# A two-network transformer kernel: where the activation tiles lie against the weight tiles, modulo 256 bytes

## Chip, cores and metric

The kernel runs on one core of one Trainium2 chip, in one launch. The metric is the device time of that launch in microseconds; the figure compared is the median of several runs.

## What is computed

Two networks run one after the other on 256 tokens of width 1024, all in float32, two layers each. Cut to what matters here:

```python
# first network, per layer (256 latent tokens; in layer 0 also 256 context tokens)
h = modulate(rmsnorm(x, norm1_g), sh1, sc1)
p = h @ w_in                                  # conv input, q, k, v, gates
y_conv = conv_branch(p[..., :GLU_END])        # depthwise conv, layernorm, silu, @ w_conv_out
y_attn = neighbourhood_attention(q, k, v) @ w_na_out
x = x + g1 * ((g_conv * y_conv + g_attn * y_attn) @ w_out)
h2 = modulate(rmsnorm(x, norm2_g), sh2, sc2)
x = x + g2 * ((silu(g) * a) @ w_down)         # a, g from dwconv(h2 @ w_up)
# second network, per layer (16 meta tokens + the 256 tokens)
u = rmsnorm_2(h) ; proj = u @ w_in
h = h + concat(indexer_attention, diff_attention, retention) @ w_out
u = rmsnorm_2(h) ; h = h + square(relu(u @ w_ff1)) @ w_ff2
```

## The kernel before

Every linear layer is done in split precision. Each float32 operand is cut into a rounded part (`_hi`) and the rest (`_lo`), and a product is three TensorE matmuls: high weights by high activations (L1369), high weights by low activations (L1370), low weights by high activations (L1374). Each of the three loads its own 128x128 weight tile and then streams 256, 272 or 512 activation columns past it. While one matmul streams, TensorE loads the weight tile of the next.

The weights come as a stream of 442 slabs of 128x1024 numbers (512 KB). A slab passes four engines, in a ring of four slots: SyncE starts its DMA into `raw`; ScalarE rounds it into `w_hi` (L846); GpSimd subtracts to get `w_lo`, in two halves (L803); TensorE uses both. TensorE's release of a slab (`slab_used`) lets ScalarE overwrite the slot of `w_hi` four slabs on, GpSimd's release (`w_lo_ready`) lets the next DMA into `raw` start. Most slabs of the first network are used by `chunk` (L1380) or `up` (L1748): for eight pieces k of the width first the L1369/L1370 pair, and when `w_lo` of the slab is there eight times L1374, so 24 matmuls a slab.

Stages of the first network, in order of time: input projection, `qk` and values of layer 0 (h, 512 columns, up to 171 us), attention of layer 0 with the gate chunks put between its steps by a table (171 to 312), the two branches (`at`, `cv`), the output mix (`y`), the up projection (`h`), the down projection (`dn`, to 766 us); then the same for layer 1 with 256 columns, apart from its key and value chunks that still have 512. In layer 1 the down projection reads `fa`. The second network starts at about 1208 us and uses `u`, `o`, `v`, `f`.

The tiles of SBUF are placed by hand: `sb` takes the next free address of a partition, rounded up to 32 bytes, `at` puts a name on any address. What counts for this change is an address modulo 256. The weight tiles of the first network (`w_hi0`, `w_lo0`) start at 128 modulo 256, and so does every 128x128 piece of them, since pieces are 512 bytes apart. In the second network the weight area has 64 bytes more in each row of pieces (`TURN`), so that successive k start 64 bytes further, as its activations of 272 columns (1088 bytes) do. Before the change a few tiles were already placed by hand 64 bytes short of the weight tiles modulo 256: `fa_hi`, `fa_lo`, and in layer 1 the copies `as_*`, `cs_*` of `at_*`, `cv_*`:

```python
fa_hi = at("fa_hi", [FF_C, SEQ], F32R, g_at + 192)
attns = [(at_hi, at_lo), (shifted("as_hi", QC, q_at, 192), shifted("as_lo", QC, q_at + QC * T_BOTH * 4, 192))]
```

Of the kernel before, what the change touches and what calls it, by code (L numbers as in the profile page):

```python
# [18 lines left out]
F32 = mybir.dt.float32  # L19
# [93 lines left out]
_n = 0  # L113
for _name, _w in (("ident", P), ("ones_d", P), ("ones_c", P), ("ones_h", P), ("perm1", P), ("perm2", P),
                  ("sel", 8), ("hsel", 16), ("sums", 2), ("cos1", SEQ), ("sin1", SEQ), ("win", GRID_W),
                  ("cos2", T2), ("sin2", T2), ("causal", N1 + N2), ("decay", 4 * 512),
                  ("onehot", VLEN), ("vmask", VLEN)):
    TAB[_name] = (_n, _n + _w)
    _n += _w
# [7 lines left out]
def build(nc, A, out, marks):  # L127
# [44 lines left out]
    with ctx:  # L172
# [28 lines left out]
        w_lo = [weight_area(f"w_lo{n}", w_at + w_size, turn) for n, turn in enumerate((0, TURN))]  # L201
        cst = sb("cst", [6 * P + 26])
        prm = sb("prm", [DEPTH, PRM1_N])
# [37 lines left out]
        x_at = top[0]  # L241
        X = sb("X", [DC, T_BOTH])
        h_at = top[0]
        h_hi = sb("h_hi", [DC, T_BOTH], F32R)
# [7 lines left out]
        ffa = at("ffa", [FF_C, T_BOTH], F32, g_at)  # L252
        fa_hi = at("fa_hi", [FF_C, SEQ], F32R, g_at + 192)
        fa_lo = at("fa_lo", [FF_C, SEQ], F32R, g_at + 192 + FF_C * SEQ * 4)
        q_at = top[0]
# [8 lines left out]
        upad = sb("upad", [CONV_C, 2, SEQ + 2 * HALO])  # L264
        top[0] += (128 - top[0]) % 256
        cv_at = top[0]
# [4 lines left out]

        def shifted(name, rows, o, by):
            return at(name, [rows, T_BOTH], F32R, o + by)[:, :, 0:SEQ]

        attns = [(at_hi, at_lo), (shifted("as_hi", QC, q_at, 192), shifted("as_lo", QC, q_at + QC * T_BOTH * 4, 192))]
        convs = [(cv_hi, cv_lo), (shifted("cs_hi", CONV_C, up_at, 192), shifted("cs_lo", CONV_C, cv_at, 192))]
        bias_at = top[0]
# [16 lines left out]
        assert 192 + 3 * DC * T2 * 4 + 4096 <= 2 * DC * T_BOTH * 4  # L294
        tab2 = at("tab2", [2 * T2 + N1 + N2 + 4 * 512], F32, x_at)
# [26 lines left out]
        assert o + 1536 + 3 * T2 * 4 <= end1, (o, end1)  # L322
        assert g_at + 192 + 2 * FF2_C * T2 * 4 <= o

# [17 lines left out]
        ident = cst[:, 0:P]  # L342
        ones_d, ones_c, ones_h = (cst[:, i * P:(i + 1) * P] for i in (1, 2, 3))
        perm1, perm2, sel = cst[:, 4 * P:5 * P], cst[:, 5 * P:6 * P], cst[:, 6 * P:6 * P + 8]
        hsel = cst[:, 6 * P + 8:6 * P + 24]
        sums = cst[:, 6 * P + 24:6 * P + 26]

# [486 lines left out]
        def _(act):  # L834
# [90 lines left out]
            def network1(layer):  # L925
# [27 lines left out]
                def attend(kind, n, *others):  # L953
# [20 lines left out]
                    elif kind == "Tx":  # L974
                        if n >= 2:
                            act.wait_ge(*after("attn_pv", (layer, n // 2 - 1)))
                        for t in range(2):
                            act.wait_ge(*after("attn_turned", (layer, n, t)))
                            copy(pt_x[n % 2][:, :, t * P:(t + 1) * P], bank[sx_bank(n, t)][:, :].rearrange("p (k q) -> p k q", k=4))\
                                .then_inc(*done("attn_pt", (layer, n, t)))  # L980
                    elif kind == "Tc" and layer == 0:
                        act.wait_ge(*after("attn_turned", (layer, n, 2)))
                        copy(pt_c[n % 2][:, :, :].rearrange("p k (t q) -> p t k q", t=2),
                             aux[2][:, :].rearrange("p (t k q) -> p t k q", t=2, k=2))\
                            .then_inc(*done("attn_pt", (layer, n, 2)))
                    elif kind == "mean":
                        for c in range(CONV_C):
                            act.wait_ge(*after("conv_centred", (layer, c)))
                            act.activation(conv_sq(c)[:, 0:T], cv[:, c, 0:T], ACT.Square).then_inc(*done("ln_sq", (layer, c)))
                    elif kind == "V":  # L990
                        act.wait_ge(*after("attn_pv", (layer, n)))
                        copy(attns[layer][0][:, n, 0:T], aux[3][:, 0:T]).then_inc(*done("attn_hi", (layer, n)))
                    elif kind == "var":

                        ahead(s + 2 * DC)
# [48 lines left out]
                for c in range(CONV_C + 1):  # L1044
# [3 lines left out]
                    if c:  # L1048
                        act.wait_ge(*after("conv_silu", (layer, c - 1)))
                        copy(convs[layer][0][:, c - 1, 0:T], nb[:, c - 1, 0:T]).then_inc(*done("conv_hi", (layer, c - 1)))  # L1050

# [294 lines left out]
        def _(pe):  # L1346
# [247 lines left out]
            def network1(layer):  # L1594
# [108 lines left out]
                def attention_branch(m):  # L1703
# [4 lines left out]
                    for k in range(4):  # L1708
                        three(bank[m % 4][:, 0:T], s + m, 4 + k, attns[layer][0][:, k, 0:T], attns[layer][1][:, k, 0:T], k == 0, k == 3)

                def conv_branch(m):
                    b = 4 + m % 4
                    claim(b)
                    for k in range(4):
                        if m == 0:
                            pe.wait_ge(*after("conv_lo", (layer, k)))
                        mm = three(bank[b][:, 0:T], s + m, k, convs[layer][0][:, k, 0:T], convs[layer][1][:, k, 0:T], k == 0, k == 3)
                    mm.then_inc(*done("slab_used", s + m))
# [529 lines left out]
        def _(dve):  # L2248
# [137 lines left out]
            def network1(layer):  # L2386
# [106 lines left out]
                def rest(p):  # L2493

                    dve.wait_ge(*after("attn_hi", (layer, p)))
                    tt(attns[layer][1][:, p, 0:T], aux[3][:, 0:T], attns[layer][0][:, p, 0:T].bitcast(F32), ALU.subtract)\
                        .then_inc(*done("attn_lo", (layer, p)))
# [51 lines left out]
                for c in range(CONV_C + 2):  # L2549
# [10 lines left out]
                    if c >= 2:  # L2560
                        dve.wait_ge(*after("conv_hi", (layer, c - 2)))
                        tt(convs[layer][1][:, c - 2, 0:T], nb[:, c - 2, 0:T], convs[layer][0][:, c - 2, 0:T].bitcast(F32), ALU.subtract)\
                            .then_inc(*done("conv_lo", (layer, c - 2)))
# [446 lines left out]
def shape_tables():  # L3010
# [9 lines left out]
    put("ones_c", np.full((P, P), 1 / (CONV_C * P)))  # L3020
    put("ones_h", (i[:, None] // HD == i[None, :] // HD) / HD)
    for name, half in (("perm1", 16), ("perm2", 32)):
# [190 lines left out]
```

## Time and profile before

| what | value |
|---|---|
| runs of the kernel before | 1958.83, 1959.35, 1960.12 us; median 1959.35 |
| profiled execution, first to last instruction | 1959.9 us (the page gives this span, and no other time of that execution; it lies 0.5 above the median, inside the three runs) |
| TensorE busy | 1904.2 us, 12126 matmuls |
| GpSimd busy | 1187.7 us |
| VectorE busy | 1065.5 us |
| ScalarE busy | 891.8 us |
| mean granted TensorE clock | 0.994 |

Matmuls overlap in the profile: the next one starts long before the modelled end of the one ahead. So the duration of a matmul isn't its price; the price is the distance from start to start, called pitch below. Engines that wait show idle time in front of an instruction and the name of what ended it; a short stall of TensorE inside a stream of matmuls shows only as a longer pitch.

### The profile page before, as it was taken

How to read it: one execution, taken by the hardware profiler on the slowest of the kernel's cores; microseconds unless marked ns; L12 is line 12 of the kernel's file. 1: busy time of each engine (PE TensorE's matmuls, PEld its weight loads, DVE VectorE, ACT ScalarE, POOL GpSimd, SP SyncE). 2: the span in 40 equal slices, each digit the busy share in tenths (PEclk: the TensorE clock that was granted, in tenths of full speed). 3: DMA queues.
4: the chain of work that ended last, by engine and by line, in shares of the span. 5: the costliest groups of instructions: out<-in, count | busy, mean ns of one | idle time of the engine just before them, and what ended most of it. 6: DMA issues, size and time to landing. Idle time of an engine off the chain costs nothing.

```text
span 1959.9 us, 33261 instructions
## 1 busy us (share of the span) xinstructions
PE 1904.2 (97%) x12126; PEld 1624.1 (83%) x12126; DVE 1065.5 (54%) x1972; ACT 891.8 (46%) x1520; POOL 1187.7 (61%) x904
## 2 busy tenths in 40 slices
PE   7999999999999999999899999999999999999998
PEld 4677777888888887877889999787999998769987
DVE  4899865354443324887657744876542048555400
ACT  4223444243443323525546645556554355555533
POOL 2444233424654554635469987674788876649986
PEclk9999999999999999999999999999999999999999
DMA  9942233628433343436465575432455564326554
GB/s 387 362 127 76 56 96 117 228 78 172 147 107 107 120 149 121 150 91 211 139 204 172 182 230 182 164 108 89 130 183 182 173 206 139 109 75 205 185 179 130
DMA packets 121541, 307.04 MB, mean 157 GB/s; under 512 B 29640, under 2 KB 51528, under 8 KB 121044
## 3 DMA queue, kind: packets, MB, share of 16 engines
q1 hardware_dynamic: 118808, 300.98, 46.8%
q10 hardware_dynamic: 2620, 4.51, 1.5%
q8 instruction: 77, 1.26, 0.3%
q14 instruction: 36, 0.29, 0.0%
HBM read 300.72 MB, written 8.06 MB: 158 GB/s over the span
## 4 chain that ended last, share of the span: by engine, by line
issue 36%; POOL 31%; PE 28%; DVE 4%; ACT 1%; POOLq 0%; ACTq 0%; DVEq 0%
POOL w_lo L803 30%; PE bank L1369 7%; PE bank L1374 6%; PE bank L1370 6%; PE bank L2081 2%; PE bank L2082 2%; PE bank L2083 2%; DVE nb L2258 1%; PE bank L1966 1%; PE bank L1968 1%; PE bank L1967 1%; ACT w_hi L846 0%; DVE v_lo L2258 0%; PE bank L2185 0%; DVE v_lo L2250 0%
## 5 line engine op out<-in xcount | busy, mean ns | idle before, releaser
L803 POOL TENSOR_TENSOR w_lo<-raw,w_hi 128x512 fp32r<-128x512 f32 x884 | 1169.7, 1353 | 759.4 <-ACT w_hi L846 757.2
L846 ACT ACTIVATE w_hi<-raw 128x1024 fp32r<-128x1024 f32 x442 | 466.1, 1056 | 285.2 <-PE bank L1374 146.8
L1369 PE MATMUL bank<-h_hi,w_hi 128*128 128x256 f32 (+1 forms) x1248 | 407.4, 342 | 1.8 <-DVE h_lo L2258 1.1
L1370 PE MATMUL bank<-h_lo,w_hi 128*128 128x256 f32 (+1 forms) x1248 | 399.4, 336 | 0.0
L1369 PEld LDWEIGHTS bank<-h_hi,w_hi 128*128 128x128 f32 x1248 | 237.2, 190 | 43.0 <-issue 13.2
L1374 PE MATMUL bank<-h_hi,w_lo 128*128 128x256 f32 (+1 forms) x1248 | 262.8, 335 | 0.0
L1370 PEld LDWEIGHTS bank<-h_lo,w_hi 128*128 128x128 f32 x1248 | 237.3, 190 | 23.6 <-issue 0.2
L1374 PEld LDWEIGHTS bank<-h_hi,w_lo 128*128 128x128 f32 x1248 | 204.7, 190 | 23.9
L1369 PE MATMUL bank<-u_hi,w_hi 128*128 128x272 f32 (+1 forms) x736 | 212.0, 288 | 1.1 <-DVE u_lo L2258 1.1
L1374 PE MATMUL bank<-u_hi,w_lo 128*128 128x272 f32 (+1 forms) x736 | 209.1, 284 | 0.0
L1370 PE MATMUL bank<-u_lo,w_hi 128*128 128x272 f32 (+1 forms) x736 | 208.3, 283 | 0.0
L1369 PEld LDWEIGHTS bank<-u_hi,w_hi 128*128 128x128 f32 x736 | 138.7, 188 | 5.5 <-issue 3.6
L1370 PEld LDWEIGHTS bank<-u_lo,w_hi 128*128 128x128 f32 x736 | 138.9, 189 | 0.1
L1374 PEld LDWEIGHTS bank<-u_hi,w_lo 128*128 128x128 f32 x736 | 138.9, 189 | 0.0
L2258 DVE SCALAR_TENSOR_TENSOR cv<-upad,prm,cv 128x512 f32<-128x512 f32 x120 | 129.0, 1075 | 3.6
L2258 DVE SCALAR_TENSOR_TENSOR up_g<-bank,prm,up_g 128x510 f32<-128x510 f32 (+1 forms) x88 | 54.2, 616 | 82.4 <-ACT up_g L1088 76.3
L2258 DVE SCALAR_TENSOR_TENSOR up_a<-bank,prm,up_a 128x510 f32<-128x510 f32 (+1 forms) x88 | 54.1, 614 | 56.4 <-ACT up_a L1088 50.4
L2250 DVE TENSOR_TENSOR bank<-bank,sq 128x272 f32<-128x272 f32 (+1 forms) x76 | 33.4, 440 | 93.3 <-ACT up_t L1296 93.2
L1369 PE MATMUL bank<-f_hi,w_hi 128*128 128x272 f32 x256 | 73.8, 288 | 0.0
L1374 PE MATMUL bank<-f_hi,w_lo 128*128 128x272 f32 x256 | 73.8, 288 | 0.0
L2258 DVE SCALAR_TENSOR_TENSOR X<-bank,gh,X 128x256 f32<-128x256 f32 x48 | 21.6, 479 | 95.3 <-PE bank L1374 95.3
L1370 PE MATMUL bank<-f_lo,w_hi 128*128 128x272 f32 x256 | 72.9, 285 | 0.0
(394 smaller groups left out, 3720.8 us busy)
## 6 DMA issues: line engine op xcount, KB each, us to landing
raw<-in_wstream SPq DMA_DIRECT2D x442, 512.0 KB, 3.5
ada_raw<-in_wada SPq DMA_DIRECT2D x48, 512.0 KB, 13.1
late_a<-in_wada SPq DMA_DIRECT2D x16, 512.0 KB, 5.1
late_b<-in_wada SPq DMA_DIRECT2D x16, 512.0 KB, 4.5
biash<-rpb_by_offset SPq DMA_DIRECT2D x64, 64.0 KB, 2.5
gates<-in_wada SPq DMA_DIRECT2D x8, 512.0 KB, 5.0
rpb_by_offset<-in_rpb SPq DMA_DIRECT2D x16, 224.0 KB
bias_by_distance<-vec ACTq DMA_DIRECT2D x1, 3264.0 KB
```

Source lines behind the costliest of these rows:

```text
L803: i = pool.tensor_tensor(lo[:, part, s, :], whole[:, part, :], hi[:, part, s, :].bitcast(F32), ALU.subtract)
L846: act.activation(w_hi[q >= first["l2", 0]][:, :, s, :], raw[:, s, :].rearrange("p (g c) -> p g c", c=PAIR), ACT.Copy)\
L1369: pe.matmul(o, tile(w_hi, i, k), a_hi, start=start, stop=False)
L1370: pe.matmul(o, tile(w_hi, i, k), a_lo, start=False, stop=False)
L1374: return pe.matmul(o, tile(w_lo, i, k), a_hi, start=False, stop=stop)
L1966: pe.matmul(lin[b][:, :], a, wh, start=kk == 0, stop=False)
L1967: pe.matmul(lin[b][:, :], al, wh, start=False, stop=False)
L2081: pe.matmul(o[:, :], hi, wh, start=j == 0, stop=False)
L2082: pe.matmul(o[:, :], lo, wh, start=False, stop=False)
L2083: return pe.matmul(o[:, :], hi, wl, start=False, stop=j == FF2_C - 1)
L2250: return dve.tensor_tensor(o, a, b, op)
L2258: return dve.scalar_tensor_tensor(out=o, in0=a, scalar=s, in1=b, op0=op0, op1=op1)
```

## The change

The constant table `ones_h` is no longer loaded (nothing read it), so `cst` is 512 bytes shorter in each partition and everything behind it starts 512 bytes lower, which changes nothing modulo 256. Then three places round the next free address up to 64 bytes short of the weight tiles modulo 256, and what was shifted by hand before is shifted no more. No instruction is added, removed or moved on any engine: the program differs in the addresses and in the width of one DMA (`cst`, 794 numbers a partition before, 666 now).

```diff
-for _name, _w in (("ident", P), ("ones_d", P), ("ones_c", P), ("ones_h", P), ("perm1", P), ("perm2", P),
+for _name, _w in (("ident", P), ("ones_d", P), ("ones_c", P), ("perm1", P), ("perm2", P),
...
-        cst = sb("cst", [6 * P + 26])
+        cst = sb("cst", [5 * P + 26])
...
         X = sb("X", [DC, T_BOTH])
+        top[0] += (w_at - 64 - top[0]) % 256
         h_at = top[0]
...
-        fa_hi = at("fa_hi", [FF_C, SEQ], F32R, g_at + 192)
-        fa_lo = at("fa_lo", [FF_C, SEQ], F32R, g_at + 192 + FF_C * SEQ * 4)
+        fa_hi = at("fa_hi", [FF_C, SEQ], F32R, g_at)
+        fa_lo = at("fa_lo", [FF_C, SEQ], F32R, g_at + FF_C * SEQ * 4)
...
-        top[0] += (128 - top[0]) % 256
+        top[0] += (w_at - 64 - top[0]) % 256
         cv_at = top[0]
...
-        attns = [(at_hi, at_lo), (shifted("as_hi", QC, q_at, 192), shifted("as_lo", QC, q_at + QC * T_BOTH * 4, 192))]
-        convs = [(cv_hi, cv_lo), (shifted("cs_hi", CONV_C, up_at, 192), shifted("cs_lo", CONV_C, cv_at, 192))]
...
         o = h_at
-        o += 192
         ffn_in = [tuple(at(f"u_{part}{l}", [DC, T2], F32R, o + by + n * DC * T2 * 4) for n, part in enumerate(("hi", "lo")))
-                  for l, by in enumerate((0, -192))]
+                  for l, by in enumerate((0, 64))]
+        o += 64
...
-                   for l, (n_mid, by) in enumerate(((T2, 192), (SEQ, 0)))]
+                   for l, (n_mid, by) in enumerate(((T2, 0), (SEQ, 64)))]
         o += (L2_FRONT * T2 + 3 * 1024) * 4
+        o += (w_at - 64 - o) % 256
```

`attns[layer][0]`, `convs[layer][0]` and their like become `at_hi`, `cv_hi` where they are used. What the code gives for the start addresses modulo 256 (the first network's weight tiles are at 128 in both; "moving" is the operand that streams):

| tile | used as | before | now |
|---|---|---|---|
| `h`, `y`; `at`, `cv` in layer 0 | moving, 256 or 512 columns | 128 | 64 |
| `h` in the value projection (L1657 to L1659) | stationary, weights move | 128 | 64 |
| `at`, `cv` in layer 1 (`as`, `cs` before) | moving, 256 columns | 64 | 64 |
| `fa` | moving, 256 columns | 64 | 64 |
| `dn` | moving, 512 columns | 128 | 128 |
| second network: `u` of its two layers | moving, 272 or 256 columns | 64, 128 | 64, 128 |
| second network: `f`; `o`, `v` of layer 0; `o` of layer 1 | | 64, 128; 64; 0 | the same |
| `qT`, `kT`, `V`, `cv`, `gates`, `pj`, the `late` loads, `ada_raw` | float32 matmuls, vector work, DMA | 128 | 64 |
| second network: `V2` | float32 matmuls | 64 | 0 |

## Rows read from the trace of the kernel before

**Rows 1.** The page, part 1: span, TensorE's busy time.

```profile
span 1959.9 us, 33261 instructions
...
PE 1904.2 (97%) x12126; PEld 1624.1 (83%) x12126; DVE 1065.5 (54%) x1972; ACT 891.8 (46%) x1520; POOL 1187.7 (61%) x904
```

**Rows 2.** Windows by stage: PE, PEld, DVE, ACT, POOL busy (instructions), PEclk, DMA, GB/s.

```profile
0.00:55.00 55.00, 40.84 (x216) 26.23 (x216) 27.49 (x56) 22.04 (x37) 10.89 (x12) 0.97 0.99 389
55.00:171.00 116.00, 116.00 (x568) 85.28 (x560) 106.00 (x132) 28.48 (x36) 59.01 (x38) 1.00 0.57 195
171.00:312.00 141.00, 135.43 (x648) 99.84 (x647) 99.00 (x176) 65.01 (x133) 46.01 (x33) 0.99 0.27 78
438.00:656.00 218.00, 218.00 (x965) 180.57 (x966) 95.32 (x129) 85.01 (x106) 114.00 (x84) 1.00 0.47 130
874.00:955.00 81.00, 75.27 (x551) 63.60 (x551) 58.72 (x128) 45.60 (x91) 41.87 (x32) 0.98 0.59 196
1031.00:1147.00 116.00, 116.00 (x969) 116.00 (x969) 86.54 (x145) 72.76 (x122) 105.70 (x81) 1.00 0.57 181
1147.00:1208.00 61.00, 60.24 (x528) 59.85 (x527) 15.82 (x19) 24.41 (x27) 55.00 (x44) 1.00 0.75 236
...
1777.00:1861.00 84.00, 84.00 (x719) 83.92 (x719) 38.71 (x94) 48.33 (x90) 76.90 (x62) 1.00 0.61 197
```

**Rows 3.** Timeline of TensorE: start, us, instruction; matmuls of one low-weight run merged.

```profile
599.91 1.98 PE L1374 MATMUL bank<-h_hi,w_lo 128*128 128x512 f32 x8
...
605.35 0.84 PE L1374 MATMUL bank<-h_hi,w_lo 128*128 128x512 f32 x3
...
1099.99 1.12 PE L1374 MATMUL bank<-h_hi,w_lo 128*128 128x256 f32 x8
...
1102.87 0.40 PE L1374 MATMUL bank<-h_hi,w_lo 128*128 128x256 f32 x2
...
1182.86 1.07 PE L1374 MATMUL bank<-fa_hi,w_lo 128*128 128x256 f32 x8
...
1185.58 0.62 PE L1374 MATMUL bank<-fa_hi,w_lo 128*128 128x256 f32 x4
```

**Rows 4.** Groups by line and form: count, busy us, mean ns of one, idle before.

```profile
L1374 PE MATMUL bank<-h_hi,w_lo 128*128 128x512 f32 x608 | 154.8, 389 | 0.0
...
L1374 PE MATMUL bank<-u_hi,w_lo 128*128 128x272 f32 x416 | 119.9, 288 | 0.0
...
L1374 PE MATMUL bank<-h_hi,w_lo 128*128 128x256 f32 x640 | 108.0, 283 | 0.0
...
L2081 PE MATMUL bank<-w_hi,f_hi 128*128 128x512 f32 x128 | 50.6, 396 | 0.0
...
L1370 PE MATMUL bank<-fa_lo,w_hi 128*128 128x256 f32 x176 | 41.0, 276 | 0.0
...
L1966 PE MATMUL bank<-w_hi,u_hi 128*128 128x512 f32 x96 | 39.4, 411 | 0.1
...
L1657 PE MATMUL bank<-w_hi,h_hi 128*128 128x512 f32 x64 | 26.0, 406 | 0.0
...
L1370 PE MATMUL bank<-as_lo,w_hi 128*128 128x256 f32 x32 | 8.8, 276 | 0.0
```

**Rows 5.** The page, part 5: the weight loads of the low-weight matmuls on h.

```profile
L1374 PEld LDWEIGHTS bank<-h_hi,w_lo 128*128 128x128 f32 x1248 | 204.7, 190 | 23.9
```

**Rows 6.** What TensorE waited for in each attention: us in total, times, longest.

```profile
PE bank L1891 <- DVE p_x L2254: 2.2, 1, 2.2
...
PE bank L1891 <- DVE sq L2254: 4.5, 6, 1.0
```

**Rows 7.** Issues of the constant table: KB, us to landing.

```profile
cst<-in_tables ACTq DMA_DIRECT2D x1, 397.0 KB, 6.5
```

**Rows 8.** GpSimd's group in the up projection of layer 1, 1031 to 1147 us.

```profile
L803 POOL TENSOR_TENSOR w_lo<-raw,w_hi 128x512 fp32r<-128x512 f32 x81 | 106.4, 1348 | 10.3 <-ACT w_hi L846 10.3
```

**Rows 9.** A window of the first attention: columns as in Rows 2.

```profile
186.00:190.00 4.00, 3.04 (x15) 2.42 (x16) 3.82 (x10) 1.82 (x4) 0.37 (x1) 0.73 0.90 344
```

More of the change, by code:

```diff
@@ L270, in build @@
         cv_lo = at("cv_lo", [CONV_C, T_BOTH], F32R, cv_at)
-        def shifted(name, rows, o, by):
-            return at(name, [rows, T_BOTH], F32R, o + by)[:, :, 0:SEQ]
-        attns = [(at_hi, at_lo), (shifted("as_hi", QC, q_at, 192), shifted("as_lo", QC, q_at + QC * T_BOTH * 4, 192))]
-        convs = [(cv_hi, cv_lo), (shifted("cs_hi", CONV_C, up_at, 192), shifted("cs_lo", CONV_C, cv_at, 192))]
         bias_at = top[0]
@@ L288, in build @@
         o = h_at
-        o += 192
         ffn_in = [tuple(at(f"u_{part}{l}", [DC, T2], F32R, o + by + n * DC * T2 * 4) for n, part in enumerate(("hi", "lo")))
-                  for l, by in enumerate((0, -192))]
+                  for l, by in enumerate((0, 64))]
+        o += 64
         H = at("H", [DC, T2], F32, o + 2 * DC * T2 * 4)
         pt_odd = at("pt_odd", [2, 512], F32, o + 3 * DC * T2 * 4)
-        assert 192 + 3 * DC * T2 * 4 + 4096 <= 2 * DC * T_BOTH * 4
+        assert 64 + 3 * DC * T2 * 4 + 4096 <= 2 * DC * T_BOTH * 4
         tab2 = at("tab2", [2 * T2 + N1 + N2 + 4 * 512], F32, x_at)
@@ L322, in build @@
         assert o + 1536 + 3 * T2 * 4 <= end1, (o, end1)
-        assert g_at + 192 + 2 * FF2_C * T2 * 4 <= o
+        assert g_at + 64 + 2 * FF2_C * T2 * 4 <= o
         KI, QI, QCR, KCR, QB, KB, QA, KA, GC = 0, 1, 5, 7, 9, 11, 13, 17, 21
@@ L342, in build @@
         ident = cst[:, 0:P]
[L343 to L346, printed above, removed]
+        ones_d, ones_c = (cst[:, i * P:(i + 1) * P] for i in (1, 2))
+        perm1, perm2, sel = cst[:, 3 * P:4 * P], cst[:, 4 * P:5 * P], cst[:, 5 * P:5 * P + 8]
+        hsel = cst[:, 5 * P + 8:5 * P + 24]
+        sums = cst[:, 5 * P + 24:5 * P + 26]
         by_distance = nc.dram_tensor("bias_by_distance", (A_HEADS + B_HEADS, P, VLEN), F32).ap()
@@ L991, in attend @@
                         act.wait_ge(*after("attn_pv", (layer, n)))
-                        copy(attns[layer][0][:, n, 0:T], aux[3][:, 0:T]).then_inc(*done("attn_hi", (layer, n)))
+                        copy(at_hi[:, n, 0:T], aux[3][:, 0:T]).then_inc(*done("attn_hi", (layer, n)))
                     elif kind == "var":
@@ L1049, in network1 @@
                         act.wait_ge(*after("conv_silu", (layer, c - 1)))
-                        copy(convs[layer][0][:, c - 1, 0:T], nb[:, c - 1, 0:T]).then_inc(*done("conv_hi", (layer, c - 1)))
+                        copy(cv_hi[:, c - 1, 0:T], nb[:, c - 1, 0:T]).then_inc(*done("conv_hi", (layer, c - 1)))
                 for m in range(DC):
@@ L1708, in attention_branch @@
                     for k in range(4):
-                        three(bank[m % 4][:, 0:T], s + m, 4 + k, attns[layer][0][:, k, 0:T], attns[layer][1][:, k, 0:T], k == 0, k == 3)
+                        three(bank[m % 4][:, 0:T], s + m, 4 + k, at_hi[:, k, 0:T], at_lo[:, k, 0:T], k == 0, k == 3)
                 def conv_branch(m):
@@ L1716, in conv_branch @@
                             pe.wait_ge(*after("conv_lo", (layer, k)))
-                        mm = three(bank[b][:, 0:T], s + m, k, convs[layer][0][:, k, 0:T], convs[layer][1][:, k, 0:T], k == 0, k == 3)
+                        mm = three(bank[b][:, 0:T], s + m, k, cv_hi[:, k, 0:T], cv_lo[:, k, 0:T], k == 0, k == 3)
                     mm.then_inc(*done("slab_used", s + m))
@@ L2495, in rest @@
                     dve.wait_ge(*after("attn_hi", (layer, p)))
-                    tt(attns[layer][1][:, p, 0:T], aux[3][:, 0:T], attns[layer][0][:, p, 0:T].bitcast(F32), ALU.subtract)\
+                    tt(at_lo[:, p, 0:T], aux[3][:, 0:T], at_hi[:, p, 0:T].bitcast(F32), ALU.subtract)\
                         .then_inc(*done("attn_lo", (layer, p)))
@@ L2561, in network1 @@
                         dve.wait_ge(*after("conv_hi", (layer, c - 2)))
-                        tt(convs[layer][1][:, c - 2, 0:T], nb[:, c - 2, 0:T], convs[layer][0][:, c - 2, 0:T].bitcast(F32), ALU.subtract)\
+                        tt(cv_lo[:, c - 2, 0:T], nb[:, c - 2, 0:T], cv_hi[:, c - 2, 0:T].bitcast(F32), ALU.subtract)\
                             .then_inc(*done("conv_lo", (layer, c - 2)))
@@ L3020, in shape_tables @@
     put("ones_c", np.full((P, P), 1 / (CONV_C * P)))
-    put("ones_h", (i[:, None] // HD == i[None, :] // HD) / HD)
     for name, half in (("perm1", 16), ("perm2", 32)):
```

## The prediction

> **What bounds the kernel now.** I read the busy times first: TensorE is busy 1904.2 of 1959.9 us [rows 1], far ahead of GpSimd, so time comes only from TensorE's stream or from its few waits. Next the windows by stage [rows 2]: in the long stages of the first network (438 to 656, 1031 to 1147 us) TensorE is busy for the whole window at a granted clock of 1.00, that is 2.4 GHz, and waits for nothing. There the only question is how far apart matmuls start.
>
> The timeline answers that [rows 3]. From one run of L1374 to the next are 24 matmuls, one slab. On h with 512 columns that takes 605.35 - 599.91 = 5.44 us, a pitch of 226.7 ns; on h with 256 columns 2.88 us, 120.0 ns; on fa with 256 columns 2.72 us, 113.3 ns. At 2.4 GHz the columns alone take 213.3 and 106.7 ns, so h pays 13.3 ns over them at both widths, and fa 6.7. The h and fa matmuls of 256 columns have the same shape, type, line and order of passes. What differs is the place: h starts at the weight tiles' own address modulo 256, fa 64 bytes before it. The durations say the same [rows 4]: 283 ns for h, 276 for fa, and also 276 for as, which a different line of code placed at the same 64 bytes. So it is the place, not the tile.
>
> While a matmul streams, the weights of the next are loaded: one load lasts 190 ns in the mean [rows 5], longer than a pitch of 113 to 120 ns, so loading and streaming read memory side by side all the time. My reading is that two streams that start at the same address modulo 256 get in each other's way once per matmul, for 6.7 ns (16 columns at 2.4 GHz, which are 64 bytes), and that 64 bytes less avoids it.
>
> The Trainium skill ("SBUF — State Buffer", section "Who interferes with whom") says against this that TensorE has two independent read ports, one for moving data and one for weight loads, and waits for no one. By that rule addresses cost nothing and the change is worth nothing; the trace disagrees at 256 columns, 120.0 against 113.3 ns, and is silent at 512.
>
> **The change part by part.** The moved tiles are h, y, and at and cv of layer 0. Per slab 24 matmuls change place. Counting with the code: at 256 columns h has 3 x 640 and y 3 x 64 = 2112 together; at 512 columns h has 3 x 608, y 3 x 64, at and cv 3 x 32 each, 2208 together (640 and 608 are in [rows 4]).
>
> *256 columns.* Price measured, 6.7 ns. Of the 2112, 1728 lie in the up projection of layer 1 (1056), the first slabs of layer 0's up projection (192), layer 1's projections (288) and its mix (192), where TensorE hardly waits: 1728 x 6.7 ns = 11.6 us. The other 384 are the gate chunks in the attention of layer 1, where TensorE is busy 75.27 of 81 us [rows 2]. They fill time between steps that end with VectorE, six of the waits for it being the 4.5 us of [rows 6]: a chunk that is done sooner then only makes the next wait longer. Of 2.6 us I take half, 1.3, with 0 and 2.6 as ends.
>
> *512 columns.* No 512-column group of the first network lies anywhere but at distance zero, so this price isn't in the trace. Its bounds: 6.7 ns if the overhead falls to that of fa; a loss if it becomes like the 512-column rows of the second network, 396 ns (L2081) and 411 ns (L1966) against 389 for h [rows 4]. I take 6.7, because the overhead over the columns is the same 13.3 ns at both widths, and because the weight load is as long as before while the streaming is longer, so that the first half of a 512-column matmul meets what a 256-column one meets. Of the 2208, 1440 lie in stages where TensorE is the bound (960 up projection of layer 0, 192 mix, 192 branches, 96 keys of layer 1): 9.6 us. 384 are the first projections of layer 0: a quarter of them runs before 55 us, where TensorE is busy only 40.84 of 55 us and the DMA engines 0.99 [rows 2], and is worth nothing; the others lie where TensorE is busy 116 of 116 us: 288 x 6.7 ns = 1.9 us. 384 are gate chunks of the first attention, busy 135.43 of 141 us, with a single wait of 2.2 us as the largest [rows 6]: of 2.6 us I take 1.5.
>
> *The value projection* (L1657 to L1659, 3 x 64 matmuls) has h as the weights, so it goes to 64 bytes on the other side. The nearest row is the up stage of the second network's layer 1, whose first two passes stream 64 bytes past their weights: 719 matmuls in 84.00 us [rows 2], 116.8 ns, 10.2 over the columns, 3 better than now. 192 x 3 ns = 0.6 us gained; ends 1.3 gained (6.7 each) and 1.3 lost (7 each, as L2081 against h).
>
> *Nothing or nearly:* fa, at and cv of layer 1, dn, u, f, o and v keep their address modulo 256. qT and kT move together. Vector, ScalarE and GpSimd operations and DMAs keep their multiples of 64 bytes; I take 0 for them. The constant load is 397 KB [rows 7] and loses 64; at the 389 GB/s of the first window [rows 2] that is 0.17 us in a DMA-bound start, of which 0.1 counted.
>
> *What is late next.* TensorE's slab in the up projection of layer 1 comes down to 24 x 113.3 ns = 2.72 us. GpSimd needs, for its two halves, 106.4 us / 40.5 slabs = 2.63 us [rows 8], 3% less, and now has 10.3 us of waits in that window to give. So it still covers, just; the fa stage shows that it can: 60.24 of 61 us busy at 113.3 ns [rows 2], though there with little VectorE work beside it. I take 1.0 us lost, between 0 and the 1056 x 6.7 ns = 7.1 us of the stage if GpSimd were the bound. The granted clock is 0.73 in a window of the first attention that follows a wait [rows 9]; about a quarter of 4 us, 1 us, is what such a drop costs. One more or one less: 0, ends -1 and +1.
>
> Sum: 11.6 + 1.3 + 9.6 + 1.9 + 1.5 + 0.6 + 0.1 - 1.0 = 25.6 us. The profiled execution's span of 1959.9 us goes to 1934.3; it lies 0.55 above the median of 1959.35, so the median goes to 1933.8. With every term at its best end (11.6 + 2.6 + 9.6 + 2.6 + 2.6 + 1.3 + 0.2 + 1.0) it would be 31.5 us, 1927.9.
>
> **The rivals.** *Only 256 columns gain.* For it: the rows of u at 64 bytes short with 272 columns take 288 ns, 174.7 over their columns, hardly less than the 175.7 of h with 512 and the 176.3 of h with 256, and not fa's 169.3 [rows 4]. There too streaming is longer than the bare columns of a 256 one. Against it: in that stage the weights move on with each k, so that the third pass streams against weights 128 bytes away, which is not so here. Then 9.6 + 1.9 + 1.5 = 13.0 us of the sum are missing: 1946.8.
>
> *512 columns lose.* They would take what the 512-column rows of the second network take, 396 x 128 and 411 x 96, 402.4 ns in the mean [rows 4], 13.4 over h. That is 2208 x 13.4 ns = 29.6 us against the 11.9 us that remain (11.6 + 1.3 - 1.0): 17.7 us slower, 1977. It decides from 5.4 ns on a matmul. Against it: those rows differ from h in the operand that moves as well as in the place.
>
> *Addresses are not the cause.* If fa and as are faster for some other reason, nothing changes: 1959.3. For it: the u rows above, at 64 bytes short and hardly faster than h. Against it: two tiles from different stages with the same 276 ns. The rule of the Trainium skill cited above ("SBUF — State Buffer", "Who interferes with whom") would make it so.
>
> **How the numbers follow.** Forecast (both widths gain) 0.74, only 256 columns 0.18, addresses not the cause 0.04, 512 columns lose 0.04. Predicted is the likeliest, 1933.8. Its own range from the ends of the terms is 1927.9 to 1942.7 (GpSimd the bound, nothing kept in the attentions). The range given goes from 1928 to 1947.5, so that it takes in the first rival. 0.2% of the time is 3.9 us, about what a measurement of this kernel can tell from no change: faster by more than that in the first two cases, 0.92; within it 0.04; slower 0.04.
>
> **What would show it.** In the profile of the changed kernel, the up projection of layer 1 should show slabs of 2.72 us and durations of 276 ns on h, and end its 116 us about 6 us sooner, with GpSimd's waits there shrinking from 10.3 us to some 4. The up projection of layer 0 should show slabs of 5.28 us (24 x 220.0 ns) and 382 ns on h with 512 columns; 5.44 us and 389 there is the first rival, over 394 the second. dn should stay at 389. The waits of both attentions should grow by a microsecond or so each. The prediction is wrong if h at 256 columns stays at 283 ns, or if GpSimd's waits vanish and TensorE starts to wait for `w_lo`.

## The result, and the profile after

The changed kernel took 1968.06 us (median of 5 runs, 1965.44 to 1974.22) against 1959.35 for the kernel before on the same chip: 1.0044 times as long, 95% interval 1.0032 to 1.0056. Forecast was 1933.8 with a range of 1928.0 to 1947.5. The change makes the kernel slower, by 0.4%. Of the rivals it is "512 columns lose", with half the price on a matmul that it was given, and with a gain at 256 columns that all but failed to come.

A word on baselines: in every later run the profiled execution's own time lies 1.9 to 2.2 us above its span (1968.06 against 1966.2 here). The span of 1959.9 before [rows 1] therefore stands for an execution of about 1962, about 2.5 above the median and not 0.5, one of the longer ones; the two spans differ by 6.3 us where the medians differ by 8.7.

The page, part 1, of the changed kernel answers to [rows 1]:

```profile
span 1966.2 us, 33261 instructions
...
PE 1906.5 (97%) x12126; PEld 1612.7 (82%) x12126; DVE 1064.3 (54%) x1972; ACT 890.9 (45%) x1520; POOL 1187.7 (60%) x904
```

The timeline of TensorE gives the pitch, as in [rows 3]; from one merged run of low-weight matmuls to the next are 24 matmuls. The line numbers shown are 3 lower than before (L1371 was L1374):

```profile
601.85 2.03 PE L1371 MATMUL bank<-h_hi,w_lo 128*128 128x512 f32 x8
...
607.45 2.03 PE L1371 MATMUL bank<-h_hi,w_lo 128*128 128x512 f32 x8
...
1061.34 1.11 PE L1371 MATMUL bank<-h_hi,w_lo 128*128 128x256 f32 x8
...
1064.17 1.11 PE L1371 MATMUL bank<-h_hi,w_lo 128*128 128x256 f32 x8
...
1104.28 1.07 PE L1371 MATMUL bank<-h_hi,w_lo 128*128 128x256 f32 x8
...
1107.00 1.07 PE L1371 MATMUL bank<-h_hi,w_lo 128*128 128x256 f32 x8
```

At 512 columns a slab of h now takes 607.45 - 601.85 = 5.60 us, 233.3 ns a matmul, where it took 5.44 us and 226.7 ns. At 256 columns there are two pitches in one stage: 2.83 us (117.9 ns) and 2.72 us (113.3 ns), where it was 2.88 (120.0) throughout. The groups by form say the same in durations, against 389 and 283 ns before [rows 4]; dn, which the change doesn't touch, stays at 389 (first the changed kernel, then dn before):

```profile
L1371 PE MATMUL bank<-h_hi,w_lo 128*128 128x512 f32 x608 | 158.7, 395 | 0.0
...
L1371 PE MATMUL bank<-h_hi,w_lo 128*128 128x256 f32 x640 | 105.2, 278 | 0.0
...
L1371 PE MATMUL bank<-dn_hi,w_lo 128*128 128x512 f32 x168 | 43.0, 389 | 0.0
```
```profile
L1374 PE MATMUL bank<-dn_hi,w_lo 128*128 128x512 f32 x168 | 43.0, 389 | 0.0
```

The windows by stage (columns as in [rows 2]), set to the stages' new times:

```profile
172.00:314.50 142.50, 136.42 (x650) 99.02 (x649) 98.78 (x176) 65.33 (x133) 46.11 (x34) 1.00 0.26 78
441.00:665.00 224.00, 224.00 (x963) 180.58 (x963) 95.33 (x129) 85.11 (x106) 114.17 (x84) 1.00 0.44 126
1039.60:1154.50 114.90, 113.50 (x963) 112.28 (x963) 85.51 (x143) 72.17 (x121) 105.07 (x81) 1.00 0.57 182
1154.50:1216.50 62.00, 60.91 (x530) 60.45 (x529) 17.07 (x20) 24.27 (x27) 55.44 (x44) 1.00 0.72 233
```

The up projection of layer 0 takes 224 us for what took 218 [rows 2]. That of layer 1 takes 114.9 us and is no longer busy throughout: TensorE idles 1.4 us of it, which it did not before. From the starts of the first matmuls of each stage in both timelines:

| stretch | before, us | after, us | difference |
|---|---|---|---|
| up to the projections of layer 0 | 55.4 | 54.8 | -0.6 |
| projections of layer 0 | 115.8 | 117.4 | +1.6 |
| attention of layer 0 | 141.4 | 142.3 | +0.9 |
| branches, mix, norm of layer 0 | 101.9 | 104.0 | +2.1 |
| first up chunks of layer 0 (192 matmuls, 256 columns) | 23.9 | 22.7 | -1.2 |
| rest of its up projection (512 columns) | 217.7 | 224.1 | +6.4 |
| down projection, norm | 129.9 | 129.9 | 0.0 |
| layer 1 up to the loop of its up projection | 245.8 | 244.4 | -1.4 |
| loop of its up projection | 115.2 | 114.9 | -0.3 |
| fa | 61.2 | 62.0 | +0.8 |
| second network, to TensorE's last matmul | 746.5 | 744.4 | -2.1 |

Layer 0 loses some 11 us where it has 512 columns; layer 1, which was to give nearly half of the gain, gives under 2. The last row is no effect of the change that can be told: in the ten later profiles whose second network lies at its old addresses modulo 256, that stretch is 1.3 to 7.4 us shorter than before as well. (`H`, its residual, moved from 64 to 128 in the changed kernel, which the table of addresses leaves out.)

### The profile page after: what moved, and what is told of

Same layout as the page of the kernel before. It is cut to its first block, busy times and chain, and to the rows that moved or that the text cites. A ratio compares the mean times of both kernels' runs of the same rounds, so it can differ in the third digit from the quotient of the medians.

```text
span 1966.2 us, 33261 instructions
## 1 busy us (share of the span) xinstructions
PE 1906.5 (97%) x12126; PEld 1612.7 (82%) x12126; DVE 1064.3 (54%) x1972; ACT 890.9 (45%) x1520; POOL 1187.7 (60%) x904
## 4 chain that ended last, share of the span: by engine, by line
issue 37%; POOL 30%; PE 27%; DVE 4%; ACT 1%; POOLq 0%; ACTq 0%; DVEq 0%
POOL w_lo L800 30%; PE bank L1366 6%; PE bank L1371 6%; PE bank L1367 6%; PE bank L2079 2%; PE bank L2078 2%; PE bank L2080 2%; DVE nb L2255 1%; PE bank L1963 1%; PE bank L1965 1%; PE bank L1964 1%; DVE v_lo L2255 1%; ACT w_hi L843 0%; PE bank L2182 0%; DVE v_lo L2247 0%
## 5 line engine op out<-in xcount | busy, mean ns | idle before, releaser
L1371 PE MATMUL bank<-h_hi,w_lo 128*128 128x256 f32 (+1 forms) x1248 | 263.9, 335 | 0.0
L1371 PEld LDWEIGHTS bank<-h_hi,w_lo 128*128 128x128 f32 x1248 | 202.3, 188 | 27.6
L1371 PE MATMUL bank<-u_hi,w_lo 128*128 128x272 f32 (+1 forms) x736 | 208.7, 284 | 0.0
L1371 PEld LDWEIGHTS bank<-u_hi,w_lo 128*128 128x128 f32 x736 | 138.5, 188 | 0.0
L1371 PE MATMUL bank<-f_hi,w_lo 128*128 128x272 f32 x256 | 73.8, 288 | 0.0
## 6 DMA issues: line engine op xcount, KB each, us to landing
ada_raw<-in_wada SPq DMA_DIRECT2D x48, 512.0 KB, 13.1
```

Of the source, the lines that this page charges most:

```text
L1371: return pe.matmul(o, tile(w_lo, i, k), a_hi, start=False, stop=stop)
```

## The experiments

Theory A: the price of a matmul hangs on the distance modulo 256 between where its streamed operand and the weight tiles start, and on its width. Theory D: in the up projection of layer 1 something other than TensorE took the gain, a ring of operations in which VectorE and ScalarE wait for each other. Where it says "before, split", the kernel is the one before without `ones_h` and with h and y named once per layer, so that each layer can lie elsewhere (`H_BY` is 0 for the old place, 192 for 64 short modulo 256):

```diff
+        H_BY = (0, 192)
+        hs = [tuple(at(f"h_{part}{l}", [DC, T_BOTH], F32R, h_at + by + n * DC * T_BOTH * 4) for n, part in enumerate(("hi", "lo")))
+              for l, by in enumerate(H_BY)]
...
-        h_raw = at("h_raw", [2 * DC, T_BOTH], F32, h_at)
+        h_raw = at("h_raw", [2 * DC, T_BOTH], F32, h_at + H_BY[1])
```

The lines of this kernel are 2 higher than before, and 3 higher where dn or the weights are moved too: L1371 or L1372 is there the pass of high weights by high activations, L1376 or L1377 that of the low weights.

**Layer 1 alone moved** (before, split, as above).

> The kernel before without ones_h, with h and y in a copy per layer: layer 0's stay at the weights' own address modulo 256, layer 1's go 64 bytes short; everything else where it was before. Theory A (the price of a matmul hangs on where its streamed operand starts against the weight tiles, and on its width: 64 bytes short costs 6.7 ns at 512 columns and gives up to 6.7 ns at 256): up projection of layer 0 back at 226.7 ns from start to start and its end back near 656 us; layer 1 from its first chunk to the second network 421 us as in the changed kernel against 422 before; together 1956 to 1960 us. Rival B (the loss comes from the other tiles that moved, V, gates, upad, cv and the loads into them, not from h): these are back as well, so the time would be the same, but then the 512-column pitch in layer 1's key chunks, where h alone is moved, would be 236 ns as before; theory A wants 241 there. Rival C (only layer 0's moves matter because of something else in layer 0): layer 1 shows no change of any pitch.

Measured: 1957.61 us, ratio 0.9996 (0.9985 to 1.0007) to the kernel before. Layer 0 is back, and the waits of TensorE in layer 1's up projection (window 1030.5 to 1145, then its timeline) show what happens there:

```profile
438.00:655.70 217.70, 217.70 (x962) 180.32 (x962) 94.97 (x129) 84.62 (x105) 114.05 (x84) 1.00 0.46 130
```
```profile
PE bank L1371 <- DVE fa_lo L2252: 2.6, 7, 0.5
```
```profile
1055.63 0.38 PE L1371 MATMUL bank<-h_hi,w_hi 128*128 128x256 f32 x1 [0.32 <-DVE fa_lo L2252]
...
1067.30 0.38 PE L1371 MATMUL bank<-h_hi,w_hi 128*128 128x256 f32 x1 [0.24 <-DVE fa_lo L2252]
...
1078.78 0.38 PE L1371 MATMUL bank<-h_hi,w_hi 128*128 128x256 f32 x1 [0.31 <-DVE fa_lo L2252]
```

So the loss is in layer 0. The key chunks of layer 1 (512 columns), where only h moved, go from 236 to 241 ns in the mean with the gaps between chunks, 227 to 233 in the median, as theory A wants; so it is h and not the tiles around it. In the up projection TensorE runs two pairs of slabs, 96 matmuls, and then waits for `fa_lo`; from one such wait to the next are 11.67 and 11.48 us, and the stage lasts 114.5 us though most of its matmuls come every 113 ns.

**Layer 0 alone moved** (before, split, `H_BY = (192, 0)`).

> The other half of the kernel with layer 1 alone moved: layer 0's h and y 64 bytes short, layer 1's at the weights' own address, the rest as before (without ones_h). Theory A: all of the loss of the changed kernel but the share of at and cv is here: the up projection of layer 0 takes 224.1 us instead of 217.7, its first chunks 21.9 instead of 23.1, y's mix 45.0 instead of 43.7, the start of dn 8 us late; layer 1 takes its 422 us as before; together 1966 to 1968.5 us. Rival B (V, gates, upad, cv and the loads into them make the loss): 1959 to 1960.

Measured: 1965.47 us, ratio 1.0029 (1.0020 to 1.0038): slower, as theory A wants, half a microsecond under the range it gave. The stage of its up projection is that of the changed kernel:

```profile
440.60:664.70 224.10, 224.10 (x962) 180.60 (x962) 95.39 (x129) 84.94 (x105) 114.23 (x84) 1.00 0.45 126
```

The two halves make +5.1 and -1.5 us by their medians. The changed kernel's +8.7 also holds at and cv of layer 0 (192 matmuls, 1.3 us by the same price). That leaves 3.8 us between three figures that are each good to some 2 us. They don't lie in layer 0: its end, the first matmul of layer 1, comes at 786.0 us before, at 794.6 here and at 795.2 in the changed kernel. Where they lie stayed open.

**Rounding of fa later** (the changed kernel with one ScalarE operation moved):

```diff
-                        if layer and w == 0 and (j or it is not None):
+                        if layer and w == 1 and (j or it is not None):
                             up_hi(j - 1, (b - 1) % 4, it)
```

> The changed kernel with one ScalarE operation of layer 1's up projection moved: the rounding of fa of the pair before (fa_hi) is done after the start operation of up_g instead of before the weight rounding ahead of it. Theory D (in that stage VectorE and ScalarE pass each pair round a ring: product into the bank, fa_hi, weight rounding, up_g, its convolution, tanh, product; it takes 5.74 us a pair whatever TensorE does, and that is what ate the gain): the ring is cut, a pair of slabs comes down to between 48 x 113.3 = 5.44 and 48 x 118 = 5.66 us, the stage from 114.9 to between 109 and 113 us, the whole to 1962 to 1966 us. Rival E (TensorE's own pitch of 118 ns or GpSimd's halves of w_lo pace the stage): the stage stays at 114 to 115 us and the whole at 1966 to 1969.

Measured: 1962.99 us, ratio 1.0016 (1.0006 to 1.0025) to the kernel before, so some 5 us under the changed kernel. The stage fell from 114.9 to 111.1 us with TensorE at 113.3 ns nearly throughout:

```profile
1041.50:1152.60 111.10, 110.49 (x962) 109.91 (x962) 90.17 (x144) 72.15 (x122) 106.24 (x81) 1.00 0.58 189
```

Theory D holds. The ring can be read in the waits; first the kernel before, 1031 to 1147 us, then the changed one, 1039.6 to 1154.5:

```profile
ACT up_t L1093 <- DVE up_g L2258: 26.0, 20, 1.8
ACT fa_hi L856 <- DVE bank L2250: 16.2, 10, 1.8
```
```profile
ACT up_t L1090 <- DVE up_g L2255: 26.0, 20, 1.8
ACT fa_hi L853 <- DVE bank L2247: 16.2, 10, 1.8
...
PE bank L1366 <- DVE fa_lo L2247: 1.3, 4, 0.4
```

ScalarE's waits for VectorE are the same to a tenth of a microsecond, although TensorE got faster: these two engines wait for each other and not for it. The groups of the changed kernel in that window give the ring's parts:

```profile
L843 ACT ACTIVATE w_hi<-raw 128x1024 fp32r<-128x1024 f32 x40 | 42.0, 1051 | 0.4
...
L1085 ACT ACTIVATE up_g<-bank,prm 128x256 f32<-128x256 f32 x20 | 11.1, 557 | 0.0
L1090 ACT ACTIVATE up_t<-up_g 128x256 f32<-128x256 f32 x20 | 8.4, 418 | 26.0 <-DVE up_g L2255 26.0
L853 ACT ACTIVATE fa_hi<-bank 128x256 f32 (+1 forms) x20 | 7.6, 381 | 16.2 <-DVE bank L2247 16.2
```
```profile
L2255 DVE SCALAR_TENSOR_TENSOR up_t<-up_t,up_g 128x256 f32<-128x256 f32 x20 | 21.9, 1096 | 9.7 <-ACT up_t L1090 9.7
L2255 DVE SCALAR_TENSOR_TENSOR up_g<-bank,prm,up_g 128x255 f32<-128x255 f32 x40 | 19.3, 483 | 12.1 <-ACT up_g L1085 9.3
...
L2247 DVE TENSOR_TENSOR bank<-up_t,up_a 128x256 f32<-128x256 f32 x20 | 18.5, 924 | 0.7
```

Round the ring for one pair of slabs: fa_hi 381 + w_hi 1051 + up_g 557 + two convolution steps 2 x 483 + tanh 418 + up_t 1096 + product 924 = 5393 ns. What a turn really takes is read from the tanh (`up_t<-up_g`), once a turn; short and long turns alternate, so four are taken together. The kernel before, the changed one, and this run:

```profile
1070.31 0.42 ACT L1093 ACTIVATE up_t<-up_g 128x256 f32<-128x256 f32 x1 [1.29 <-DVE up_g L2258]
...
1093.47 0.42 ACT L1093 ACTIVATE up_t<-up_g 128x256 f32<-128x256 f32 x1 [1.29 <-DVE up_g L2258]
```
```profile
1071.67 0.42 ACT L1090 ACTIVATE up_t<-up_g 128x256 f32<-128x256 f32 x1 [1.29 <-DVE up_g L2255]
...
1094.78 0.42 ACT L1090 ACTIVATE up_t<-up_g 128x256 f32<-128x256 f32 x1 [1.29 <-DVE up_g L2255]
```
```profile
1084.58 0.42 ACT L1090 ACTIVATE up_t<-up_g 128x256 f32<-128x256 f32 x1 [1.88 <-DVE up_g L2255]
...
1106.55 0.42 ACT L1090 ACTIVATE up_t<-up_g 128x256 f32<-128x256 f32 x1 [1.88 <-DVE up_g L2255]
```

That is 5.79 us a turn before and 5.78 in the changed kernel, as in the waits of TensorE above (11.67 + 11.48 us for four turns), and not the 5.74 that the expectations give. It leaves 0.4 us a turn for the hand-overs between the engines. TensorE itself took 48 x 120.0 ns = 5.76 us a turn before: the two bounds lay on each other. With the rounding moved a turn takes 5.49 us, near TensorE's 48 x 113.3 ns = 5.44: what cutting the ring gives hangs on the pitch that TensorE then runs at.

**The kernel before with the same rounding moved** (split, `H_BY = (0, 0)`).

> The kernel before, addresses untouched, with only the rounding of fa of the pair before put behind the start operation of up_g. Theory D says that a pair of slabs took TensorE 48 x 120.0 = 5.76 us there, 0.02 more than the ring of VectorE and ScalarE, so that both bounds lay on each other: with the ring cut TensorE's 5.76 stay, the stage stays 115 us and the whole 1958 to 1960. Rival H (the ring alone paced the stage before as well): the stage falls to 111 us and the whole to about 1955 without any move of an address.

Measured: 1958.22 us, ratio 0.9990 (0.9981 to 1.0000); the stage took 115.9 us at 120.0 ns a matmul, and a turn 5.76 us (tanh at 1092.63 and, four turns on, at 1115.67), which is TensorE's own time. So cutting the ring alone gives nothing that can be told, and neither does moving h of layer 1 alone: each uncovers the other.

**Both together** (layer 1 alone moved, and the rounding moved).

> Both edits together: layer 0's h and y at the weights' own address modulo 256, layer 1's 64 bytes short, and the rounding of fa of the pair before put behind the start operation of up_g. Theory A and D: layer 0 as in the kernel before (up projection 217.7 us), the up projection of layer 1 at 113.3 to 118 ns a matmul and without the waits of 0.6 us that TensorE has there every 96 matmuls with layer 1 alone moved: that stage 109 to 113.5 us against 114.5, the whole 1951 to 1956 us, against 1957.6 with layer 1 alone moved. Rival E (the stage falls only because something else in the changed kernel was late): no gain over 1957.6.

Measured: 1954.33 us (1949.58 to 1956.51), ratio 0.9971 (0.9960 to 0.9983): faster than both kernels. But the stage of the profiled execution missed what was said:

```profile
1029.90:1144.00 114.10, 113.19 (x963) 112.99 (x963) 81.16 (x146) 73.66 (x122) 106.54 (x81) 1.00 0.57 185
```
```profile
1100.61 1.10 PE L1376 MATMUL bank<-h_hi,w_lo 128*128 128x256 f32 x8
...
1103.44 1.10 PE L1376 MATMUL bank<-h_hi,w_lo 128*128 128x256 f32 x8
```

TensorE waited only 0.9 us, once, but ran nearly all of the stage at 2.83 us a slab, 117.9 ns. The ring's turn went with it, 5.65 us (tanh at 1084.61 and, four turns on, at 1107.22). The same distance gave 2.72 us in the run above with the rounding moved. At 64 short there are two steady pitches, and in these profiles a change from one to the other comes only where the stream is interrupted, though not every interruption brings one. In the changed kernel the stage runs at 118 ns from 1042 to 1099 us, at 113 to 1139, then at 118 again, and each change comes at a stall. What decides between them stayed open.

Nor does the stage make most of the gain in this profile. Its span is 9.2 us under that of the kernel before: fa starts 3.0 us sooner and takes 1.0 longer, and from the start of the second network to TensorE's last matmul are 7.2 us less, though no distance was changed there. What fa has to do with that is tested below.

**The scan of distances** (before, split, each one profiled run, so only pitches count). In the first, dn is 64 short as well: `dn_hi = at("dn_hi", [2, 512], F32R, nb_at + 192)` and its like; in two also fa was moved.

> h and y of both layers 64 bytes past the weight tiles modulo 256, and dn, which neither kernel moves, 64 bytes short of them; the rest as before. Theory A: dn goes from 226.7 to 233.3 ns from start to start and its stage, 110.3 us, gets 3.4 us longer (504 x 6.7). For h at +64 it gives no number; the value projection of the changed kernel, which streams weights past h at this distance with 512 columns, took 225 to 229 ns, so 512 columns of h should be near 227 and the time about 1963. Rival F (any distance but zero costs 512 columns 6.7 ns): h at 512 columns 233 ns, time about 1974 to 1978. If dn stays at 226.7 ns, theory A is wrong and h's loss had another cause.

> h and y of both layers, and dn, 128 bytes away from the weight tiles modulo 256 (half way round); the rest as before. If two streams clash only where they are near each other modulo 256, this is the farthest place and both widths should be at their cheapest: 512 columns at 220 ns or less and 256 at 113.3, so about 2200 x 6.7 + 504 x 6.7 = 18 us off layer 0 and some more off layer 1: 1935 to 1942. Rival F (any distance but zero costs 512 columns 6.7 ns): 233 ns on h and dn, about 1974 to 1978. Rival G (64 bytes is the only place that differs): 226.7 and 120.0 as before, 1959.

> The distances at 32 bytes: h and y of both layers 32 past the weight tiles modulo 256, dn and fa 32 short; the rest as in the kernel before. So far over the bare columns: 13.3 ns at 0 for both widths; 17 to 23 (512) and 6.7 or 11.3 (256) at 64 short; 13 to 19 and 6.7 to 11.3 at 64 past; 16 to 28 and 8 to 15 at 128. If the price is a matter of 64-byte pieces, 32 bytes straddle two of them and cost at least what the dearer neighbour does: 512 columns 13 to 23, 256 columns 11 to 13, time 1960 to 1970. If it goes smoothly with the distance, 32 lies between 0 and 64: h at 512 columns 227 to 229 ns, h at 256 between 113.3 and 120, time about 1958 to 1963.

> The distances at 96 bytes: h and y of both layers 96 short of the weight tiles modulo 256, dn and fa 96 past; the rest as in the kernel before. By the values at 64 and 128 on either side: h at 512 columns 231 to 237 ns, time 1968 to 1976; dn between 226.7 and 233; h and fa at 256 columns 113.3 to 120. A 512-column pitch below 226.7 on any of these tiles would show that zero is not the best place for this width.

Slabs of 24 matmuls from their timelines, in us (nanoseconds a matmul):

| distance of the streamed operand | 512 columns | 256 columns |
|---|---|---|
| 0 (before) | 5.44 (226.7) | 2.88 (120.0) |
| 32 past | 5.60 (233.3) | 2.80 (116.7) |
| 64 past | 5.49 (228.8) | 2.83 (117.9) |
| 96 past (dn, fa) | 5.60 (233.3) | 2.88 (120.0) |
| 128 | 5.58 (232.5) | 2.85 (118.8) |
| 96 short | 5.63 (234.6) | 2.81 (117.1) |
| 64 short | 5.60 (233.3) | 2.72 or 2.83 (113.3 or 117.9) |
| 32 short (dn, fa) | 5.60 (233.3) | 2.84 (118.3) |

The totals were 1965.53 (64 past), 1969.93 (128), 1967.68 (32) and 1970.76 (96). dn at 64 short, the direct test on a tile that neither kernel moves:

```profile
713.87 2.03 PE L1377 MATMUL bank<-dn_hi,w_lo 128*128 128x512 f32 x8
...
719.47 2.03 PE L1377 MATMUL bank<-dn_hi,w_lo 128*128 128x512 f32 x8
```

5.60 us where the changed kernel has 5.44 on dn, and the stretch from dn to layer 1 went from 129.9 to 133.2 us: the 3.4 that were expected. The idea that the farthest place is the cheapest fell at 128, and that of a smooth course fell at 32. For 512 columns distance zero is the best of the eight places. For 256 columns the five others that h was put at are better than zero; fa at 96 past is no better and at 32 short hardly (its stages take 63.5 and 63.4 us there, and 63.3 at zero, below). Why a distance costs what it does no run shows.

**Weights moved, activations not** (before, split with `H_BY = (0, 0)`, and the weight tiles 64 bytes on):

```diff
         raw = sb("raw", [RING, SLAB])
+        top[0] += 64
         w_at = top[0]
```

> The kernel before with the weight tiles 64 bytes on (at 192 modulo 256) and the activations where they were (without ones_h, with h and y in a copy per layer at the same place). Every distance of the first network falls by 64: h, y, at, cv and dn to 64 short, fa and layer 1's as and cs to 128; in the second network u to 128 and 0, the others likewise. Theory A (only the distance counts): h and dn at 512 columns 231 to 236 ns as with the activations moved, up projection of layer 0 224 us; h at 256 columns 113.3 or 118; fa 115 to 122. Rival K (the activation's own address counts, 64 modulo 256 being bad for 512 columns): h and dn stay at 226.7 ns, h at 256 columns at 120.

Measured: 1973.32 us. The up projection of layer 0, with h at its old address:

```profile
602.06 2.03 PE L1377 MATMUL bank<-h_hi,w_lo 128*128 128x512 f32 x8
...
607.66 2.03 PE L1377 MATMUL bank<-h_hi,w_lo 128*128 128x512 f32 x8
```

5.60 us again, and dn likewise (714.73 to 720.33). At 256 columns most slabs of h in layer 1 take 2.72 or 2.83 us, as with h moved to 64 short, and most of fa, now 128 away, 2.85, as h at 128. It is the distance that counts, not the activation's own address. Nor does it matter which operand is the activation: in the value projection, where the weights stream past h, the median distance between starts is 227 ns at zero, 229 where the weights are 64 past h and 233 where they are 64 short of it (h at 64 past, in the first scan).

**fa at the weights' own address** (the kernel before, `g_at + 192` made `g_at` for `fa_hi` and `fa_lo`).

> The kernel before with one edit: fa at the weights' own address modulo 256 instead of 64 bytes short. Theory A: fa's 528 matmuls go from 113.3 to 120.0 ns, its stage from 61.2 to about 63.4 us. Theory I (where fa goes slower, the weight stream gets farther ahead of TensorE, and the second network then starts without the waits for v_lo and w_lo and the granted clock of 0.50 behind them: its first two slabs' worth of v took 17 to 18.6 us in the profiles with fa at 113.3 at its end and 13.0 to 13.3 in those with fa at 118): v's stretch falls from 18.0 to 13.3 us, together 1956 to 1957.5 us. Rival J (v's stretch falls by chance, or with other edits): v's stretch stays at 17 to 18 and the whole goes to 1961 to 1962.

Measured: 1958.28 us, ratio 0.9998 (0.9989 to 1.0007). First the kernel before, then this one, fa's stage and the first projection of the second network (columns as in [rows 2]):

```profile
1147.00:1208.20 61.20, 60.44 (x530) 60.05 (x529) 16.02 (x19) 24.41 (x27) 55.00 (x44) 1.00 0.75 235
1208.20:1226.20 18.00, 15.92 (x99) 14.74 (x99) 15.17 (x21) 13.62 (x28) 9.07 (x7) 0.81 0.38 117
```
```profile
1148.00:1211.30 63.30, 63.30 (x530) 63.30 (x529) 16.92 (x27) 27.13 (x32) 56.66 (x46) 1.00 0.71 229
1211.30:1223.50 12.20, 12.20 (x99) 12.00 (x98) 11.48 (x14) 9.88 (x21) 6.64 (x5) 1.00 0.50 167
```

In these two profiles slower matmuls make the whole shorter: fa takes 2.1 us more, the stretch behind it 5.8 less, without its waits and at a granted clock of 1.00 where it was 0.81. The timed runs don't confirm the sum: 0.9998 is no gain that can be told, and the expected 1956 to 1957.5 us did not come. By its span the profiled execution of the kernel before was a long one, but its 18.0 us are not unusual. In the seven profiles where fa ends at 113.3 ns a matmul, the first 96 matmuls of the second network take 16.6 to 18.4 us from the first start to the last; in the six where fa ends at 117.8 to 120.0, they take 12.1 to 13.1. With fa's stage that is 78.4 to 81.0 us against 75.2 to 76.6 (the run with moved weights is left out, since its second network has other distances).

**All of it** (layer 1 moved, rounding moved, fa at the weights' own address).

> Layer 0 at the weights' own address, layer 1's h and y 64 bytes short, the rounding of fa behind up_g, and fa at the weights' own address. Theories A, D and I together: fa's stage 63.4 us in every execution instead of 60 to 62, v's stretch 13.3 us in every one; up projection of layer 1 as with both edits, 109 to 114 us by which of its two pitches it falls into; the whole 1952 to 1956 us, not far from the 1954.3 without this edit, but with a narrower spread. Rival J: 1956 to 1959.

Measured: 1952.33 us (1950.51 to 1952.64), ratio 0.9962 (0.9949 to 0.9976): in the expected range and the lowest ratio of all, though its interval overlaps that of the run without fa moved (0.9960 to 0.9983). The spread was narrow, 2.1 us in 5 runs against 6.9 in 7 without fa moved on another chip; that fa brings this is not shown, since with fa alone moved 11 runs spread over 4.5 us. Its profile has fa and the stretch behind it at 63.3 and 12.3 us:

```profile
1139.60:1202.90 63.30, 63.30 (x531) 63.30 (x529) 16.93 (x26) 27.16 (x32) 57.00 (x46) 1.00 0.71 229
1202.90:1215.20 12.30, 12.27 (x99) 12.05 (x98) 11.58 (x14) 9.88 (x21) 6.79 (x5) 1.00 0.50 165
```

## Why the prediction was wrong

- **The bound, and that places set the price: right.** TensorE is the bound in the long stages, pitches decide, and the place modulo 256 sets them; moving the weights instead of the activations shows that it is the distance. The Trainium skill ("SBUF — State Buffer", section "Who interferes with whom") has TensorE's two read ports independent, by which all of this would cost nothing; the runs disagree at both widths, 226.7 against 233.3 ns and 120.0 against 113.3.
- **The mechanism, and with it 512 columns, 6.7 ns gained: the step that failed.** The prediction took it that two streams at the same address modulo 256 get in each other's way once per matmul, at either width. At 512 columns the same address is the cheapest of the eight places tried. It took fa's price over "because the overhead over the columns is the same 13.3 ns at both widths". The measured price is 6.7 ns lost, 220.0 forecast and 233.3 found. The terms of 9.6, 1.9 and 1.5 us became losses: +6.4 in the up projection alone (960 x 6.7), +1.6 in the first projections, +0.9 in the first attention, and most of +2.1 in branches and mix. The rows that pointed there, 396 and 411 ns in the second network [rows 4], were set aside since they differ from h in more than the place; the rival built on them had the right sign and took 13.4 ns for 6.7. Whether those rows are slow for their place no run shows.
- **256 columns, 11.6 us: half right, then covered.** The first chunks of layer 0, 192 matmuls, gave 1.2 us where 1.3 was due. In layer 1 the tiles that moved, h and y, ran at about 118 ns more often than at 113.3 (1108 of their 256-column distances between starts are 116 to 120 ns, 746 are 111 to 115). That is a second steady pitch, which fa hardly shows in the profile of the kernel before; in two later profiles, the two with h of layer 1 at 64 short, the rounding moved and fa left, fa ran at it throughout from the same place.
- **What is late next: the wrong engine.** The prediction asked whether GpSimd could keep up with a slab of 2.72 us and took 1.0 us off. GpSimd kept its 10.3 us of waits. The bound was the ring of VectorE and ScalarE at 5.79 us a pair, beside TensorE's 5.76: of 6.4 us 0.3 came. With the ring cut the stage took 111.1 us in one profile and 114.1 in another, by which of the two pitches it ran at. The ring stood in the trace of before, as 26.0 and 16.2 us of waits between two engines that don't look busy (86.54 and 72.76 of 116 us [rows 2]).
- **Attentions: the direction right, the size not.** In layer 1 the waits for VectorE's `sq` grew by 0.4 us (4.9 after 4.5 [rows 6]) where a microsecond was said, and the stretch gained 0.5 us where 1.3 was; in layer 0 there was nothing to keep, as its gate chunks have 512 columns.
- **Value projection, 0.6 us: not gained.** Its matmuls in layer 0 come every 229 ns after 227 (21 of them from 146.92 to 151.73 us), so some 0.3 us are lost, inside the ends given.
- **`ones_h`, clock:** nothing that the trace tells from zero.
- **Slips that change nothing here:** the upper end of its own range leaves out the lost 1.3 us of the value projection and the 1 us of the clock, with which it is about 1945.5 and not 1942.7; and 72 of the first projections' 384 matmuls start before 55 us, not a quarter.

## What to carry to other kernels

A price measured at one width is no price at another: before a layout is turned to it, move one tile of each width (here dn would have done for 512 columns) and read the pitch. And where a stage's bound is taken away, the next one is not the busiest engine but the longest ring: add up, for one turn of the loop, the durations of the operations that wait for each other across engines, and compare with the bound's own time per turn. Waits that stayed the same to a tenth of a microsecond when the bound got faster were the mark of it here.

## What was not expected of the hardware

- One address layout gave two steady pitches, 113.3 and 117.9 ns, in the same stage of the same run, each held over dozens to hundreds of matmuls and changed only at a stall; at distance zero every slab of 256 columns without a stall showed one, 120.0.
- At 512 columns every one of seven other distances, 32 to 128 bytes, costs 2 to 8 ns more than zero; at 256 columns six cost 1 to 7 ns less and one, 96 past, the same.
- Two operations of the ring in which VectorE reads both inputs from SBUF hang on when GpSimd runs. In the changed kernel the product took 1.41 us and `up_t` 1.54 with GpSimd's subtractions beside them throughout (at 1108.30 and 1106.73 us), 0.43 and 0.71 us with GpSimd beside them for 0.18 and 0.43 us (at 1102.63 and 1101.89). The convolution steps between, which read a PSUM bank, took 0.48 us each beside GpSimd. Long and short turns of the ring, 6.65 and 4.85 to 5.0 us, alternate with it.
